# A decoder step on one core: order of the loads and of the first projections in the front

## What is computed

```python
proj = x @ w_in                       # 1024 x 2568: u, q, k, v, o (512 each), gi, gf (4 each)
u, q, k, v, o, gi, gf = split(proj)
pool_out, hist_new = pool_mix(u, hist, pos0, w_pool, pool_scale)
ig = gi + b_i
lf = log_sigmoid(gf + b_f)
h, C, n, m = mlstm(q, k, v, ig, lf, C0, n0, m0)      # chunks of 128 tokens
h = sigmoid(o) * head_norm(h, mh_g)
x1 = LN1(alpha * x + concat(pool_out, h) @ w_out)
ff = moe(x1)                          # top 4 of 32 experts, softmax router, clamped SwiGLU
x2 = LN2(alpha * x1 + ff)
y  = x2 + sigmoid(x2 @ w_ple_gate) * (p @ w_ple)
```

## Time and profile before

| | us |
|---|---|
| median of 3 runs | 1200.85 (1199.71 to 1201.38) |
| span of the profiled execution | 1200.0 |
| TensorE busy | 1084.2 (90%) |
| VectorE busy | 282.8 (24%) |
| ScalarE busy | 145.7 (12%) |
| GpSimd busy | 99.3 (8%) |

### The profile page before, as it was taken

How to read it: one execution, slowest core, us unless ns; L and a number is a source line. 1 busy time by engine, 2 the same in 40 slices (tenths; PEclk the granted TensorE clock), 3 DMA queues, 4 the chain that set the end, 5 groups by cost and what they waited for, 6 DMA issues and landing times.

```text
span 1200.0 us, 13601 instructions
## 1 busy us (share of the span) xinstructions
PE 1084.2 (90%) x5054; PEld 430.8 (36%) x5054; DVE 282.8 (24%) x657; ACT 145.7 (12%) x232; POOL 99.3 (8%) x119
## 2 busy tenths in 40 slices
PE   7899989999999999989898988989999988998878
PEld 4678463333333222232223222222222222222233
DVE  1455881111111111111111111111111111111174
ACT  1332121011000100010001000100010001000022
POOL 1523530000000000000000000000000000000000
PEclk9899978999999999999999999999999999999989
DMA  9953696999999999999999999999999999999860
GB/s 311 294 203 150 216 375 243 418 417 417 418 419 417 417 418 418 418 418 418 418 418 418 417 418 418 418 418 417 418 417 418 418 418 417 418 418 418 338 250 37
DMA packets 91295, 448.51 MB, mean 374 GB/s; under 512 B 11929, under 2 KB 12821, under 8 KB 57618
## 3 DMA queue, kind: packets, MB, share of 16 engines
q1 hardware_dynamic: 83536, 439.00, 90.7%
q0 software_dynamic: 3680, 8.04, 1.9%
q10 hardware_dynamic: 4057, 1.20, 0.5%
HBM read 440.33 MB, written 12.16 MB: 377 GB/s over the span
## 4 chain that ended last, share of the span: by engine, by line
SPq 37%; PE 29%; DMA 26%; issue 3%; DVE 3%; ACTq 1%; ACT 1%; POOLq 0%; DVEq 0%
SPq L349 37%; DMA ring<-in_w_mlp 24%; PE bank L764 8%; PE bank L486 5%; PE bank L791 4%; PE bank L862 3%; PE bank L734 2%; PE bank L637 2%; DMA small<-in_b_f 1%; ACTq L1325 1%; DMA ring<-ff_rows 1%; PE bank L731 1%; SPq L387 1%; DVE scol L974 1%; PE bank L741 0%
## 5 line engine op out<-in xcount | busy, mean ns | idle before, releaser
L764 PE MATMUL bank<-ring,proj 128*64 128x512 f32 x2048 | 473.5, 600 | 73.4 <-DMA ring<-in_w_mlp 73.4
L764 PEld LDWEIGHTS bank<-ring,proj 128*64 128x64 f32 x2048 | 135.0, 136 | 394.1 <-DMA ring<-in_w_mlp 194.6
L791 PE MATMUL bank<-ring,wpool 128*64 128x512 f32 x1024 | 225.2, 592 | 0.0
L1231 DVE TENSOR_SCALAR proj<-bank 128x256 f32<-128x256 f32 x64 | 24.2, 419 | 504.6 <-PE bank L764 504.6
L791 PEld LDWEIGHTS bank<-ring,wpool 128*64 128x64 f32 x1024 | 72.5, 137 | 130.9 <-issue 128.9
L1605 POOL DMA_INDIRECT ff_rows<-mixT,erow x32 | 31.5, 983 | 929.8 <-ACT mixT L1469 929.8
L734 PE MATMUL bank<-xreg,proj 128*64 128x512 f32 (+1 forms) x396 | 99.7, 622 | 0.0
L1460 ACT ACTIVATE proj<-proj 128x512 f32<-128x512 f32 x32 | 20.2, 632 | 551.2 <-DVE proj L1231 551.2
L486 PE MATMUL bank<-xT,ring 128*128 128x264 f32 x320 | 77.6, 402 | 4.7 <-ACT proj L1334 4.7
L1203 DVE TENSOR_TENSOR proj<-cst,proj 128x384 f32<-128x384 f32 x33 | 18.4, 559 | 230.8 <-ACT mixT L1469 230.1
L486 PEld LDWEIGHTS bank<-xT,ring 128*128 128x128 f32 x320 | 62.9, 199 | 17.1 <-ACT proj L1334 5.1
(11 more groups left out here) (281 smaller groups left out, 591.2 us busy)
## 6 DMA issues: line engine op xcount, KB each, us to landing
ring<-in_w_mlp SPq DMA_DIRECT2D x384, 1024.0 KB, 21.9
ring<-in_w_in SPq DMA_DIRECT2D x10, 1024.0 KB, 17.0
ring<-in_w_out SPq DMA_DIRECT2D x4, 1024.0 KB, 10.8
ring<-in_w_ple_gate SPq DMA_DIRECT2D x4, 1024.0 KB, 13.4
ring<-ff_rows SPq DMA_DIRECT2D x4, 1024.0 KB, 12.7
xreg<-in_x_prompt SPq DMA_DIRECT2D x4, 512.0 KB, 5.5
ring<-q_row SPq DMA_DIRECT2D x1, 2048.0 KB, 7.0
ring<-k_row SPq DMA_DIRECT2D x1, 2048.0 KB, 7.3
```

The lines of the kernel that those rows point to most:

```text
L764: last = pe.matmul(bank[q][BLOCK * t:BLOCK * (t + 1), :], xgT[:, k % 4, k // 4, :], ring[:, s, col:col + 512], start=False, stop=(k == KD ...
L791: last = pe.matmul(bank[4][BLOCK * h:BLOCK * (h + 1), :], aT[:, m, BLOCK * t:BLOCK * (t + 1)], w[:, k % 2, 512 * h:512 * h + 512], start=F ...
L1231: TS(glu[:, q, :], hb[q][:, 0, :], LIMIT, None, ALU.min).then_inc(sem("glu_ready"), 1)
```

## The change

The constants are loaded in two parts, the identity (128 columns) first, and TensorE waits for that part alone; VectorE, ScalarE and GpSimd wait for the rest where they first need it. All other loads leave ScalarE's queue: wgate, b_i, b_f and hist go on SyncE's queue behind block 0, n and m behind block 1, w_pool, pool_scale and mh_g behind block 4, w_router and b_router behind C. On TensorE the gate projection moves behind tiles 0 and 1, tile 2 follows it, then the two small gate matmuls, the history sums and tile 3. ScalarE evicts tile 1 ahead of the gates' activation. VectorE evicts tile 2 ahead of the gates' copy, and copies the history sums behind the first two steps of the softplus.

```diff
--- before.py
+++ after.py
@@ -311,7 +311,15 @@
                                  .rearrange("(k p) n -> p k n", p=P)).then_inc(sem(f"slot{s}"), 16)
 
             load_block(0)
+            sp.dma_start(wgate[:, :, :], w_in[0, :, 2560:2568].rearrange("(k p) n -> p k n", p=P))\
+              .then_inc(sem("gate_in"), 16)
+            sp.dma_start(gbias[0:HEADS, :], b_i.rearrange("o h -> h o")).then_inc(sem("gate_in"), 16)
+            sp.dma_start(gbias[HEADS:2 * HEADS, :], b_f.rearrange("o h -> h o")).then_inc(sem("gate_in"), 16)
+            sp.dma_start(hist[0:SAMPLES * HIST, :], state_pool[0].rearrange("b r d -> (b r) d"))\
+              .then_inc(sem("hist_in"), 16)
             load_block(1)
+            sp.dma_start(srow[:, SN, :], state_n[0].rearrange("b h k -> (b h) k")).then_inc(sem("states_in"), 16)
+            sp.dma_start(s_col[S_M0], state_m.rearrange("o b h -> (b h) o")).then_inc(sem("states_in"), 16)
             load_block(2)
 
             for g in range(3):
@@ -320,7 +328,12 @@
                 sp.dma_start(bsrc[rows_, 2 * FF:3 * FF], b_mlp2[0]).then_inc(sem("bias_in"), 16)
             load_block(3)
             load_block(4)
+            sp.dma_start(wpool[:, :, :], w_pool[0].rearrange("g c d -> c g d")).then_inc(sem("pool_in"), 16)
+            sp.dma_start(pscale, pool_scale[0].rearrange("(g d) -> d g", d=P)).then_inc(sem("pool_in"), 16)
+            sp.dma_start(mhg, mh_g[0].rearrange("(g d) -> d g", d=P)).then_inc(sem("pool_in"), 16)
             sp.dma_start(Cst, state_C[0].rearrange("b h v k -> v (b h) k")).then_inc(sem("cq_in"), 16)
+            sp.dma_start(wrout[:, :, :], w_router[0].rearrange("(k p) e -> p k e", p=P)).then_inc(sem("wrout_in"), 16)
+            sp.dma_start(brout[:, :], b_router).then_inc(sem("wrout_in"), 16)
 
             def load_w_out(s):
                 sp.wait_ge(sem("tile_ps"), 4 * (s // 2) + 4)
@@ -445,7 +458,7 @@
 
         @block.tensor
         def _(pe):
-            pe.wait_ge(sem("cst_in"), 16)
+            pe.wait_ge(sem("ident_in"), 16)
 
             for g in range(6):
                 c, half = g // 2, g % 2
@@ -459,19 +472,6 @@
 
             pe.wait_ge(sem("xT_dve"), 3)
             pe.wait_ge(sem("xT_act"), 3)
-            pe.wait_ge(sem("gate_in"), 48)
-            for k in range(KD):
-                last = pe.matmul(bank[6][0:2 * HEADS, 0:TOK], wgate[:, k, :], xT[:, k, :],
-                                 start=(k == 0), stop=(k == KD - 1))
-            last.then_inc(sem("gates_ps"), 1)
-
-            pe.wait_ge(sem("hist_in"), 16)
-            for g in range(4):
-                last = pe.matmul(bank[7][:, g * SAMPLES:(g + 1) * SAMPLES], hist[0:SAMPLES * HIST, g * P:(g + 1) * P],
-                                 cst[0:SAMPLES * HIST, C_HIST + g * SAMPLES:C_HIST + (g + 1) * SAMPLES],
-                                 start=True, stop=True)
-            last.then_inc(sem("hist_ps"), 1)
-
             def project(t):
                 b, j = t // 4, t % 4
                 if t >= 2:
@@ -531,14 +531,29 @@
                 last.then_inc(sem("hT_ps"), 1)
 
             project(0)
+            project(1)
+
+            pe.wait_ge(sem("gate_in"), 48)
+            for k in range(KD):
+                last = pe.matmul(bank[6][0:2 * HEADS, 0:TOK], wgate[:, k, :], xT[:, k, :],
+                                 start=(k == 0), stop=(k == KD - 1))
+            last.then_inc(sem("gates_ps"), 1)
+            project(2)
 
             pe.wait_ge(sem("gates_done"), 1)
+            pe.wait_ge(sem("spread_ready"), 1)
             pe.matmul(bank[5][0:HEADS, 0:SEQ], ident[0:2 * HEADS, HEADS:2 * HEADS], gates[:, 0:SEQ],
                       start=True, stop=True)
-            pe.wait_ge(sem("spread_ready"), 1)
             pe.matmul(bank[5][0:STATES, SEQ:SEQ + 2], s_spread, cst[0:2 * HEADS, C_KIND:C_KIND + 2],
                       start=True, stop=True).then_inc(sem("gates_ps"), 1)
-            for t in range(1, 6):
+
+            pe.wait_ge(sem("hist_in"), 16)
+            for g in range(4):
+                last = pe.matmul(bank[7][:, g * SAMPLES:(g + 1) * SAMPLES], hist[0:SAMPLES * HIST, g * P:(g + 1) * P],
+                                 cst[0:SAMPLES * HIST, C_HIST + g * SAMPLES:C_HIST + (g + 1) * SAMPLES],
+                                 start=True, stop=True)
+            last.then_inc(sem("hist_ps"), 1)
+            for t in range(3, 6):
                 project(t)
 
             pe.wait_ge(sem("hist_done"), 1)
@@ -908,9 +923,6 @@
                 dve.wait_ge(sem("xT_ps"), g + 1)
                 dve.tensor_copy(xT[:, 0:4, t0:t0 + n], bank[g][:, :].rearrange("p (k t) -> p k t", k=4)[:, :, 0:n])\
                    .then_inc(sem("xT_dve"), 1)
-            dve.wait_ge(sem("hist_ps"), 1)
-            dve.tensor_copy(histsum, bank[7][:, 0:32]).then_inc(sem("hist_done"), 1)
-
             def empty_tile(t):
                 dve.wait_ge(sem("tile_ps"), t + 1)
                 if T_K <= t < T_V:
@@ -925,16 +937,19 @@
                 ins.then_inc(sem(name), 1)
 
             empty_tile(0)
+            dve.wait_ge(sem("cst_in"), 16)
             dve.wait_ge(sem("gates_done"), 1)
             step(TT(s_spread.rearrange("g (b h) -> g b h", h=HEADS),
                     gates[:, SEQ:TOK].unsqueeze(2).to_broadcast([2 * HEADS, SAMPLES, HEADS]),
                     cst[0:2 * HEADS, C_HEAD:C_HEAD + STATES].rearrange("g (b h) -> g b h", h=HEADS), ALU.mult),
                  "spread_ready")
 
+            empty_tile(2)
             dve.wait_ge(sem("gates_ps"), 2)
             step(dve.tensor_copy(fgate[:, :], bank[5][0:HEADS, 0:SEQ]))
             step(STT(softp, fgate[:, :], -1.0, fgate[:, :], ALU.mult, ALU.min), "soft_ready")
-            empty_tile(2)
+            dve.wait_ge(sem("hist_ps"), 1)
+            dve.tensor_copy(histsum, bank[7][:, 0:32]).then_inc(sem("hist_done"), 1)
             dve.wait_ge(sem("soft_done"), 1)
             step(STT(logf, fgate[:, :], 0.0, softp, ALU.min, ALU.subtract))
             for c in range(2):
@@ -1298,14 +1313,8 @@
         @block.scalar
         def _(act):
 
-            act.dma_start(cst[:, :], consts).then_inc(sem("cst_in"), 16)
-            act.dma_start(wgate[:, :, :], w_in[0, :, 2560:2568].rearrange("(k p) n -> p k n", p=P))\
-               .then_inc(sem("gate_in"), 16)
-            act.dma_start(gbias[0:HEADS, :], b_i.rearrange("o h -> h o")).then_inc(sem("gate_in"), 16)
-            act.dma_start(gbias[HEADS:2 * HEADS, :], b_f.rearrange("o h -> h o")).then_inc(sem("gate_in"), 16)
-
-            act.dma_start(hist[0:SAMPLES * HIST, :], state_pool[0].rearrange("b r d -> (b r) d"))\
-               .then_inc(sem("hist_in"), 16)
+            act.dma_start(ident, consts[:, C_ID:C_ID + P]).then_inc(sem("ident_in"), 16)
+            act.dma_start(cst[:, C_ID + P:C_END], consts[:, C_ID + P:C_END]).then_inc(sem("cst_in"), 16)
 
             for g in (1, 3, 5):
                 c = g // 2
@@ -1313,17 +1322,6 @@
                 act.wait_ge(sem("xT_ps"), g + 1)
                 act.copy(xT[:, 4:8, t0:t0 + n], bank[g][:, :].rearrange("p (k t) -> p k t", k=4)[:, :, 0:n])\
                    .then_inc(sem("xT_act"), 1)
-            act.wait_ge(sem("gates_ps"), 1)
-            act.wait_ge(sem("gate_in"), 48)
-            act.activation(gates[:, :], bank[6][0:2 * HEADS, 0:TOK], ACT.Identity, bias=gbias).then_inc(sem("gates_done"), 1)
-            act.dma_start(srow[:, SN, :], state_n[0].rearrange("b h k -> (b h) k")).then_inc(sem("states_in"), 16)
-            act.dma_start(s_col[S_M0], state_m.rearrange("o b h -> (b h) o")).then_inc(sem("states_in"), 16)
-            act.dma_start(wpool[:, :, :], w_pool[0].rearrange("g c d -> c g d")).then_inc(sem("pool_in"), 16)
-            act.dma_start(pscale, pool_scale[0].rearrange("(g d) -> d g", d=P)).then_inc(sem("pool_in"), 16)
-            act.dma_start(mhg, mh_g[0].rearrange("(g d) -> d g", d=P)).then_inc(sem("pool_in"), 16)
-            act.dma_start(wrout[:, :, :], w_router[0].rearrange("(k p) e -> p k e", p=P)).then_inc(sem("wrout_in"), 16)
-            act.dma_start(brout[:, :], b_router).then_inc(sem("wrout_in"), 16)
-
             def empty_tile(t):
                 act.wait_ge(sem("tile_ps"), t + 1)
                 if t >= 16:
@@ -1334,10 +1332,14 @@
                     ins = act.copy(proj[:, t, :], bank[t % 2][:, 0:TOK])
                 ins.then_inc(sem("tile_act"), 1)
 
+            empty_tile(1)
+            act.wait_ge(sem("gates_ps"), 1)
+            act.wait_ge(sem("gate_in"), 48)
+            act.activation(gates[:, :], bank[6][0:2 * HEADS, 0:TOK], ACT.Identity, bias=gbias).then_inc(sem("gates_done"), 1)
             one = ones[0:HEADS, 0:1]
             act.wait_ge(sem("soft_ready"), 1)
             act.activation(softp, softp, ACT.Exp).then_inc(sem("soft_exp"), 1)
-            empty_tile(1)
+            act.wait_ge(sem("cst_in"), 16)
             act.wait_ge(sem("soft_exp"), 1)
             act.activation(softp, softp, ACT.Ln, bias=one).then_inc(sem("soft_done"), 1)
```

(1 more changed line is left out.)

## The result

| | before | after |
|---|---|---|
| median of 6 runs, us | 1201.12 (1199.71 to 1202.75) | 1195.03 (1187.55 to 1196.79) |
| profiled execution: time, us | not recorded | 1187.55 |
| profiled execution: span, us | 1200.0 | 1185.7 |

The ratio is 0.9936 (95% interval 0.9914 to 0.9958): faster by 6 us where 15 were forecast, and above the range. The profiled execution, however, is the fastest of the six, and its span is the forecast's 1185.0 within 0.7 us. Both facts have to be explained. First the profile after, for that one execution.

The account below looks back on a forecast made before the run. TensorE bounds the front, and the end stands at a fixed distance behind the first expert's start; 11.05 + 4.6 - 0.65 = 15.0 us off gives span 1185.0, plus 0.85 forecast 1185.9; range 1182.5 to 1192.

Parts of the forecast that it names:

- the range: Whole kernel's time: 1182.5 to 1192 us, leaving out rivals B and C, no change at all and the edges.
- ScalarE's queue: Front: loads off ScalarE and tile 1 evicted early save 4.7 us of wait and 2.5 of slow tiles, 7.2 us.
- Rival C: ScalarE's queue not the cause: its blocked time reappears elsewhere in the front; 1197 us, chance 0.03.
- The gate projection: TensorE's front: moved behind tiles 0 and 1, saves 3.0 us wait and 1.9 us slow matmul, less 0.3 for block 0.
- rows_ready: Gate chain on ScalarE and VectorE: ready at 38.3 us; TensorE waits 0.75 us, transposed rows come 11.05 us earlier.
- q_row and the product: SyncE's load and GpSimd's product: q_row issued at 52.5 us behind DMA's backlog, product from 66.3 to 75.2 us.
- It is no longer held: VectorE's scol copy L974 comes at 63.05 us, before GpSimd's product at 66.3; gives back 2.9 and 1.7 us.
- third wait: TensorE's wait for VectorE's scol copy L974: 2.9 us, with 1.7 us of slow tile behind it, counted as won.
- rival A: Lock stays expensive: third wait stays, or L1009 held 3 us more; gain 11 or 12, time 1189.5, chance 0.25.
- The step from span to median: Whole kernel: 0.85 us added to the span of 1185.0 for a forecast of 1185.9 us.
- Rival B: SyncE's queue: small runs at 100 ns cost 6.4 us a set, delaying q_row and product 17 us; 1205, chance 0.04.
- Rival D: Near the first expert, 180 to 190 us: clock rises ahead of the last gathers; time 1183 us, chance 0.10.

Follow-up runs that it names:

- loads_only: Against the kernel before: small loads moved to SyncE's queue as in the change, constants whole and program orders as before; 1196.42 us, ratio 0.9961.
- again3: The kernel after, unchanged, run again; median 1194.05 us of 3 executions, the profiled one 1193.04 us.
- best_warm2: Kernel after plus: GpSimd's product behind sdiag, tile 6 between the score matmuls, rest of constants behind block 0, four matmuls of zeros; 1184.82 us, ratio 0.9868.
- late: Kernel after with TensorE repeating the gate matmul, 3.6 us more work; 1195.86 us.
- behind: Kernel after with GpSimd's product also waiting for VectorE's sdiag; 1189.3 us.
- warm: Kernel after plus four matmuls of zeros around the transposes; 1185.74, 1186.28, 1186.3, 1186.78 and 1192.01 us.
- best_warm: Kernel after plus: GpSimd's product behind sdiag, tile 6 between the score matmuls, rest of constants behind block 0, eight matmuls of zeros; 1186.74 us, ratio 0.9878.

## Why the prediction was right and wrong

*ScalarE's queue: right.* ScalarE is no longer idle by issue in the front, tile 3 doesn't wait, and tiles 3 to 5 take 10.78 us. `loads_only` shows the removal alone, at 4.9 us of the 7.2; 1.7 of the rest is the longer wait for b_f. The long issues haven't gone, they stand on SyncE now, and no wait of TensorE's in the front hangs on them: w_router's takes 6.95 us there. Rival C falls with it: a queue that cost nothing would have brought nothing. The Trainium skill says that the issue time saved by using several engines is usually small beside the DMA ("DMA: Bandwidth & Descriptors", Issuing engines are not separate DMA queues). This case is an exception, now by a run and no longer by a row alone.

*The gate projection: right in kind, one term too small.* The gate matmul took 3.66 us (forecast 3.56) without waiting, but it ended at 22.86 us and not at 21.5. Tiles 0 and 1 were priced at full clock, 3.56 us each, with 0.3 us for block 0's second half, and took 8.97 us. The half landed near 13.3 us and not at 12.6, towards the slow end of the bounds (11.8 to 13.5). In the profile after that costs almost no wait, because TensorE worked at half speed until then; in `again3` it did not, and waited 1.14 us. With the constants behind block 0 (`best_warm2`) the half is there at 12.34, and the wait is 0.36 us.

*rows_ready: right to 0.7 us, in part by luck.* L562 started at 38.96 us (forecast 38.3). VectorE's L972 ended at 38.82, close to the forecast, but TensorE didn't wait 0.75 us for it: it came 1.4 us later than forecast, at 38.94. Its slow start had used up that wait, and the 0.65 us forecast at L601 as well. So the two forecast waits, 1.4 us in all, stand in for the slow tiles that the sum left out.

*q_row and the product: right in place.* It was issued at 53.13 us (forecast 52.5) and started the product at 66.37 us (66.3). DMA's backlog sets it, as forecast: in `late` q_row is issued 3.5 us later, at 56.65, and the product starts no later, at 64.96. In the profile after, L601 is at 77.12 (77.2), the first expert at 173.75 (173.6), and the span 1185.7 us (1185.0).

*"It is no longer held": the step that failed.* The sum takes the product at 66.3 and L974 (L989 after) at 63.05, and books the whole third wait, 2.9 + 1.7 us, as won. Two things are wrong with it. First, the margin was counted from L974 only. VectorE goes on at once to L1002 (L1017 after), which can be held as well; rival A and the signs of being wrong name it, but "both edges are 3 us away" is not true of it. By the prediction's own numbers it ends at 63.05 + 0.2 + 1.3 = 64.5, 1.8 us ahead of the product; in the profile after the margin is 1.28 us. Second, only the product's start was given an uncertainty (2 us), while TensorE's own time was read off one execution as if it were fixed. The runs show it to vary by 1.5 to 1.7 us at each of two places, and the product's start by 2.0 us over seven profiles. Such a margin doesn't hold against both, and in 12 of 21 executions, by their times, it didn't; of the one of them that was profiled, `again3`, the trace shows it.

*Rival A: the right mechanism, mis-sized and under-rated.* Its name was "the lock stays expensive", with 0.25. It was priced at 3 to 4 us, from the third wait kept or a later end of L1009. The measured price of L1017 held is 6.6 us at L601 (83.73 against 77.12): 1.4 us by which TensorE was late already, 3.4 us of its wait for L1021, and some 1.8 us of slow work behind it (L593 takes 3.29 us and not 1.95). From heap to heap it is 7.9 us by the means, from span to span of the two profiles 5.4 us (1191.1 against 1185.7). The median lies in the upper heap, so the time was 1195.0 and not A's 1189.5. The Trainium skill's page "SBUF — State Buffer" (Who interferes with whom), by which the two engines share one pair of ports under an exclusive lock, agrees: VectorE's operation on SBUF waited to the end of GpSimd's, 9.93 us for 1.29.

*The range: one heap only.* It was the range of one execution's course, 1182.5 to 1192. All nine executions of the lower heap are in it, and none of the twelve of the upper one. The step from span to median (0.85 us) is mis-sized too: from its own span an execution's time is 1.85 us away, so 1 us of the miss is here. And it supposed that the profiled execution stands for the median; of this kernel the profiled ones were 1187.55, 1188.3, 1187.22 and 1193.04.

*Rival B: fell.* On SyncE's queue the sets of 1024 small runs cost about what they did before: the product starts where forecast, DMA moved 226 GB/s with a share of 1.20 in the stretch that has the second set, and only 288 packets remain on ScalarE's queue.

```profile
q10 hardware_dynamic: 288, 0.51, 0.1%
...
42.00:44.00 2.00, 2.00 (x10) 1.71 (x10) 0.98 (x4) 1.25 (x4) 1.71 (x5) 1.00 1.20 226
```

Two such microseconds at 226 instead of 384 GB/s lose 0.8 us, not 6.4. *Rival D* didn't show in the kernel after: L779's first group took 15.58 us (15.00 before). Its mechanism, the clock's rise ahead of the last gathers, is what `best_warm2` has (4.47 us for L749).

## What to carry to other kernels

Where an operation is "no longer held", look for the next one behind it on the same engine, and write down the margin in microseconds against how much the kernel's own engines vary between executions; if the margin is smaller, the gain is a matter of chance, and a wait that orders the two operations makes it sure. What that wait itself costs these runs can't tell: `behind` has 1185.73 to 1190.62, the lower heap 1184.01 to 1190.15. Run a kernel several times and look at the list of times, not the median alone: two heaps can mean a threshold, and one profile shows only one side of it. A reordering and the loads that feed it are to be judged together, since here the new order alone lost 4 us, the loads alone won 5, and both together won 10 in the same comparison.

## What the runs showed of the hardware

The granted clock of the same instructions at the same time differs between executions: 0.51 and 1.00 from 42.5 to 45.9 us behind small matmuls. Tiles 0 and 1 take from 8.74 to 10.34 us behind the transposes, by the time for which their matmuls last 0.64 and not 0.39 us each, though the clock column reads 1.00 there. With four matmuls of zeros (`warm`, `best_warm2`) and with eight (`best_warm`) the profiled execution ran them at 0.39 us from the first; whether that makes the executions of `warm` faster, five of them don't show, and eight delayed the transposes. VectorE's operations on SBUF were held to the end of a GpSimd product of 8.85 us: 9.93 us for 1.29 (`again3`), 6.62 for 0.19 (`late`), 7.17 for 0.28 (after); one that had begun before the product ran on undisturbed (0.687 us, `again3`). And a DMA issue isn't always cheap: an issue of 0.1 KB held ScalarE for 9.37 us before, and with the order changed alone ScalarE was still idle by issue for 13.5 us, on the path of two other engines.
